# Output projection of a hybrid encoder trunk: seven block products in place of eight in half of the k pairs of five weight groups

## The reference, cut to what matters

```python
for l in range(DEPTH):                       # 2 layers, 1024 tokens, D_MODEL 2048, float32
    h = rmsnorm(x, norm_gain[l])
    proj = einsum('bsd,de->bse', h, w_in[l])     # q, k, v, g_attn, x_rnn, g_rnn
    attn = swa_sink_attention(q, k, v, sinks[l], cos, sin)
    rnn = rg_lru(causal_conv(x_rnn, ...), ...)
    mixed = concatenate([attn * silu(g_attn), rnn * silu(g_rnn)])    # 2048 wide
    x = x + einsum('bse,ed->bsd', mixed, w_out[l])                   # the change is here
return rmsnorm(x, final_gain)
```

## Time and profile before

| what | value |
|---|---|
| median of 3 runs | 2317.74 us (2317.38 to 2317.77) |
| the profiled execution | 2318.04 us |
| its span, first to last instruction | 2316.0 us |
| TensorE busy | 2308.8 us, 12970 matmuls |
| VectorE busy | 1443.1 us |
| ScalarE busy | 1270.0 us |

### The profile page before, as it was taken

The page is one execution under the profiler, slowest core; times in us unless marked ns, Lnnn a source line. Parts: engine busy times, 40 slices in busy tenths (PEclk is TensorE's granted clock), DMA queues, the critical chain, the costliest instruction groups (busy, mean ns, idle before and its releaser), DMA issues.

```text
span 2316.0 us, 34189 instructions
## 1 busy us (share of the span) xinstructions
PE 2308.8 (100%) x12970; PEld 1896.7 (82%) x12970; DVE 1443.1 (62%) x2307; ACT 1270.0 (55%) x2435; POOL 0.8 (0%) x10
## 2 busy tenths in 40 slices
PE   9999999999999999999999999999999999999999
PEld 8888888888888888888888888888888888888888
DVE  7668777434546877744475786764355478776335
ACT  7558566324456767534465676653244557665333
POOL 0000000000000000000000000000000000000000
PEclk9999999999999999999999999999999999999999
DMA  5334323333332233353334533233333333223333
GB/s 194 103 110 149 94 89 94 98 96 100 91 103 87 85 96 88 100 168 95 98 107 146 177 104 94 89 96 97 100 95 96 94 94 89 87 89 100 96 98 140
DMA packets 127028, 244.62 MB, mean 106 GB/s; under 512 B 14352, under 2 KB 18704, under 8 KB 126096
## 3 DMA queue, kind: packets, MB, share of 16 engines
q1 hardware_dynamic: 126288, 242.28, 33.5%
q10 hardware_dynamic: 576, 0.16, 0.0%
HBM read 234.00 MB, written 8.39 MB: 105 GB/s over the span
## 4 chain that ended last, share of the span: by engine, by line
PE 97%; DVE 2%; ACT 1%; issue 1%; POOL 0%; ACTq 0%; POOLq 0%
PE proj L417 91%; PE ps_at L497 1%; PE ps_at L522 1%; PE ps_at L541 1%; PE proj L433 1%; DVE wcut L979 0%; PE proj L460 0%; DVE xc L1175 0%; DVE xcut L1189 0%; DVE prob L1149 0%; ACT wcut L618 0%; ACT prob L753 0%; PE ps_at L393 0%; ACT sqr L790 0%; ACT sqr L792 0%
## 5 line engine op out<-in xcount | busy, mean ns | idle before, releaser
L417 PE MATMUL proj<-operand,wcut 128*128 128x512 f32 x9480 | 2183.4, 391 | 0.0
L417 PEld LDWEIGHTS proj<-operand,wcut 128*128 128x128 f32 x9480 | 1775.3, 188 | 380.6 <-issue 11.0
L979 DVE TENSOR_TENSOR wcut<-wraw,wcut 128x512 fp32r<-128x512 f32 x804 | 554.3, 690 | 802.8 <-ACT wcut L618 799.7
L618 ACT ACTIVATE wcut<-wraw 128x512 fp32r<-128x512 f32 x803 | 506.3, 631 | 915.2 <-PE proj L417 890.0
L753 ACT ACTIVATE prob<-ps_at,stat 128x128 f32<-128x128 f32 x256 | 89.9, 363 | 0.8
L701 ACT ACTIVATE gy<-proj 32x512 f32<-32x512 f32 x144 | 84.9, 590 | 3.8
L658 ACT ACTIVATE sqr<-x 128x512 f32<-128x512 f32 x62 | 36.8, 635 | 45.4 <-DVE x L1220 45.2
L1008 DVE TENSOR_TENSOR acc<-acc,sqr 128x512 f32<-128x512 f32 x80 | 55.2, 691 | 4.9 <-ACT sqr L658 0.2
L764 ACT ACTIVATE mixed<-ps_at 64x256 f32<-64x256 f32 x128 | 48.6, 379 | 14.3 <-PE ps_at L522 11.9
L753 ACT ACTIVATION_READ_ACCUMULATOR prob<-ps_at,stat 128x1 f32 x256 | 51.8, 202 | 0.0
L1175 DVE SCALAR_TENSOR_TENSOR xc<-xr,pars,xc 128x512 f32<-128x512 f32 x64 | 47.9, 749 | 1.4
(11 more groups left out here) (154 smaller groups left out, 1193.0 us busy)
## 6 DMA issues: line engine op xcount, KB each, us to landing
wraw<-in_w SPq DMA_DIRECT2D x804, 256.0 KB, 2.6
x<-in_xt SPq DMA_DIRECT2D x2, 4096.0 KB, 13.5
mixed<-in_xt SPq DMA_DIRECT2D x14, 512.0 KB, 7.4
gw<-in_gates SPq DMA_DIRECT2D x32, 128.0 KB, 2.6
out<-x SPq DMA_DIRECT2D x4, 1024.0 KB, 4.9
out<-mixed SPq DMA_DIRECT2D x7, 512.0 KB, 2.6
tab<-in_cossin SPq DMA_DIRECT2D x8, 256.0 KB, 3.3
mixed<-in_xt SPq DMA_DIRECT2D x4, 256.0 KB, 3.4
```

Source lines behind the costliest of these rows:

```text
L417: last = pe.matmul(bank[:, :], wcut[:, u % RING, a, c:c + P], operand[:, k, b, :], start=(k == 0 and n == 0), stop=(k == KT - 1 and n == 2))
L618: act.activation(wcut[:, u % RING, 0, :], wraw[:, u % RING, :], ACT.Copy).then_inc(w_hi, 1)
L979: dve.tensor_tensor(wcut[:, u % RING, 1, :], wraw[:, u % RING, :], wcut[:, u % RING, 0, :].bitcast(F32), ALU.subtract).then_inc(w_lo, 1)
```

## The change

Groups 19 to 23 of each layer treat four of their eight k pairs (`NSP` = 4) as a 2x2 block product: two k blocks by two output tiles, times two k blocks by two halves of 256 tokens. Eight block products of 256 tokens become seven (Strassen's form as arranged by Winograd), each still three fp32r matmuls. Four of the seven (`lead`) need sums of weight blocks and of operand blocks, and are made during the group before, in the other pair of banks; then ScalarE and VectorE add the banks across (`lead_copy_out`, `lead_sums`), and the plain k pairs and the other three products (`cross_part`) gather on top. A slot that has a cross part with it is in `SIDES`.

Group 18 has twelve slots (144 to 155): four of them, every second one, are lead parts for group 19. Groups 19 to 22 have eight each: in slots 2 to 5 of a group TensorE makes a cross part of its own group and a lead part of the next, the other four are plain. Group 23 has four plain slots, each with a cross part. So slots stay 200.

For each such k pair VectorE makes five sums of 128x128 weight blocks (`weight_sums`) in place in the raw ring, three slots ahead, before `weight_hi` may round them; two raw blocks are loaded once more (`cross`, 128 KB), and cut to high and low beside one of the sums (`cross_cut_hi`, `cross_cut_lo`), two slots ahead. The operand sums are made once per layer and half, at slots 126, 128, 136 and 143. The next half's x is loaded in two parts, at slots 148 and 195. Several buffers share memory with ones that are idle in this stage (left out below, with declarations and the index helpers).

```diff
--- before
+++ after
@@ -61,7 +61,33 @@
 STREAM = [(g, j) for j in range(5) for g in range(2)] + [(g, j) for g in range(2) for j in range(5, UPG)]
-STREAM += [(g, j) for g in range(2, PG + OG) for j in range(UPG)]
+STREAM += [(g, j) for g in range(2, PG) for j in range(UPG)]
+KIND = ["plain"] * len(STREAM)
+SIDE = [None] * len(STREAM)
+NSP = 4
+SG = list(range(PG + 2, PG + 7))
+def out_slots():
+    for g in range(PG, PG + OG):
+        plain = list(range(NSP if g in SG else 0, UPG))
+        for s in range(UPG + (g + 1 == SG[0]) * NSP - (g == SG[-1]) * NSP):
+            ahead = s - 2 if g in SG else (s - 2) // 2
+            if g + 1 in SG and ahead in range(NSP) and (g in SG or s % 2 == 0):
+                yield "ahead", g + 1, ahead, (g, ahead) if g in SG else None
+            else:
+                yield "plain", g, plain.pop(0), (g, s) if g == SG[-1] else None
+OSTART = [None] * OG + [SLOTS]
+for what, g, j, side in out_slots():
+    at = g - PG - (what == "ahead")
+    if OSTART[at] is None:
+        OSTART[at] = len(STREAM)
+    STREAM.append((g, j))
+    KIND.append(what)
+    SIDE.append(side)
...
-XS = O0 + (OG - 1) * UPG + 1
+XS = OSTART[OG - 1] + 1
+PIECE = {STREAM[s]: s for s in range(SLOTS) if KIND[s] == "ahead"}
+SIDES = [s for s in range(SLOTS) if SIDE[s]]
+NPC = len(PIECE)
+CUTS = 3
+HOLD = 5
+T_AT = (126, 128, 136, 143)
...
@@ -358,10 +428,25 @@
                             sp_.wait_ge(gw_lo, h * (DEPTH * RT) + (n + 1))
                             sp_.dma_start(gw[:, n % GRING, :, :], gates[l, j]).then_inc(gw_in[n % GRING], 16)
+                        if s + 1 in SIDES:
+                            g, i = SIDE[s + 1]
+                            n = at_piece(h, l, piece(g, i))
+                            sp_.wait_ge(xsum_lo, per_layer(h, l, NSP, 1))
+                            if n >= HOLD:
+                                sp_.wait_ge(cross_lo, n - HOLD + 1)
+                            sp_.dma_start(cross[n % HOLD][:, 0:2 * P],
+                                          w[l, PIECE[g, i], :, 2 * P:4 * P]).then_inc(cross_in[n % HOLD], 16)
                         if l == 1 and s == O0 + 12 and h < LAST:
                             sp_.wait_ge(op_lo, at_op(h, 1, 1, KT - 1))
-                            for i in range(KT // 2):
+                            sp_.wait_ge(xsum_done, per_layer(h, 1, NSP, NSP))
+                            for i in range(KT // 4):
+                                x_load(h + 1, i)
+                        if l == 1 and s == OSTART[OG - 1] + AHEAD and h < LAST:
+                            sp_.wait_ge(unit_done, at_unit(h, 1, OSTART[OG - 1] - 1))
+                            for i in range(KT // 4, KT // 2):
                                 x_load(h + 1, i)
...
@@ -401,6 +486,8 @@
                 if s == 0:
                     pe.wait_ge(evac, h * (DEPTH * TILES) + (l * TILES + 2))
+                if g in SG and s == OSTART[g - PG]:
+                    pe.wait_ge(lead_done, 3 * (lead_at(h, l, g) + 1))
                 pe.wait_ge(w_lo, h * UNITS + (u + 1))
...
@@ -410,13 +497,47 @@
                         bank = proj[2 * ((l * (PG + OG) + g) % 2) + m]
                         c = kk * GW + m * P
                         for n, (a, b) in enumerate(((0, 0), (0, 1), (1, 0))):
-                            if (kk, m, n) == (KU - 1, 1, 2) and s + 1 < SLOTS and STREAM[s + 1][1] == 0:
+                            if ((kk, m, n) == (KU - 1, 1, 2) and s + 1 < SLOTS and STREAM[s + 1][1] == 0
+                                    and KIND[s + 1] == "plain"):
                                 pe.wait_ge(evac, h * (DEPTH * TILES) + (l * TILES + 2 * STREAM[s + 1][0] + 2))
                             last = pe.matmul(bank[:, :], wcut[:, u % RING, a, c:c + P], operand[:, k, b, :],
-                                             start=(k == 0 and n == 0), stop=(k == KT - 1 and n == 2))
-                last.then_inc(unit_done, 1)
+                                             start=(k == 0 and n == 0), stop=(k == KT - 1 and n == 2),
+                                             skip_group_check=g in SG)
+                return last
+            def lead(h, l, s):
+                u = l * SLOTS + s
+                g, i = STREAM[s]
+                k1 = KU * i
+                banks = bank_of(l, 2 * g), bank_of(l, 2 * g + 1)
+                if i == 0:
+                    pe.wait_ge(evac, h * (DEPTH * TILES) + (l * TILES + 2 * g + 2))
+                if g == SG[0]:
+                    pe.wait_ge(xsum_lo, per_layer(h, l, NSP, i + 1))
+                pe.wait_ge(w_lo, h * UNITS + (u + 1))
+                for c, b, m, half in ((0, None, 0, 0), (3, 1, 0, 1), (2, 2, 1, 0), (1, 0, 1, 1)):
+                    for n, (hi, lo) in enumerate(((0, 0), (0, 1), (1, 0))):
+                        src = operand[:, k1, lo, 0:HT] if b is None else xsum[i][:, lo, b, :]
+                        last = pe.matmul(banks[m][:, HT * half:HT * half + HT], wcut[:, u % RING, hi, P * c:P * c + P],
+                                         src, start=(i == 0 and n == 0 and half == 0),
+                                         stop=(i == NSP - 1 and n == 2), skip_group_check=True)
+                return last
+            def cross_part(h, l, g, i):
+                n = at_piece(h, l, piece(g, i))
+                k2 = KU * i + 1
+                pe.wait_ge(cross_lo, n + 1)
+                cut = crosscut[n % CUTS]
+                for c, b, m, half in ((0, 0, 0, 0), (2, 1, 0, 1), (1, None, 1, 0)):
+                    for hi, lo in ((0, 0), (0, 1), (1, 0)):
+                        src = operand[:, k2, lo, HT * b:HT * b + HT] if b is not None else xsum[i][:, lo, 3, :]
+                        last = pe.matmul(bank_of(l, 2 * g + m)[:, HT * half:HT * half + HT], cut[:, hi, P * c:P * c + P],
+                                         src, start=False, stop=False, skip_group_check=True)
+                return last
...
@@ -549,7 +670,13 @@
                         elif h == 0 and l == 0 and s == 0:
                             first_units()
                         elif h > 0 or l > 0 or s > 1:
-                            unit(h, l, s)
+                            if KIND[s] == "plain":
+                                last = unit(h, l, s)
+                            if SIDE[s]:
+                                last = cross_part(h, l, *SIDE[s])
+                            if KIND[s] == "ahead":
+                                last = lead(h, l, s)
+                            last.then_inc(unit_done, 1)
                         if h > 0 and l == 0 and s == SS_OUT:
                             sum_of_squares(h - 1, DEPTH)
...
@@ -615,7 +742,31 @@
                     act.wait_ge(unit_done, u - RING + 1)
                 if u == 1:
                     act.wait_ge(w_hi, 1)
+                if u < TOTAL and KIND[u % SLOTS] == "ahead":
+                    act.wait_ge(wsum_done, at_piece(u // UNITS, u // SLOTS % DEPTH, piece(*STREAM[u % SLOTS])) * 2 + 2)
                 act.activation(wcut[:, u % RING, 0, :], wraw[:, u % RING, :], ACT.Copy).then_inc(w_hi, 1)
+            def cross_cut_hi(h, l, g, i):
+                n = at_piece(h, l, piece(g, i))
+                act.wait_ge(cross_in[n % HOLD], 16 * (n // HOLD + 1))
+                act.wait_ge(wsum_done, 2 * n + 2)
+                if n >= CUTS:
+                    hb, r = divmod(n - CUTS, DEPTH * NPC)
+                    act.wait_ge(unit_done, at_unit(hb, r // NPC, SIDES[r % NPC]))
+                act.activation(crosscut[n % CUTS][:, 0, :], cross[n % HOLD], ACT.Copy).then_inc(cross_hi, 1)
+            def xsum_cut_hi(h, l, i):
+                act.wait_ge(xsum_done, per_layer(h, l, NSP, i + 1))
+                if i >= 2:
+                    act.wait_ge(op_lo, at_op(h, l, 1, AT + RT // 2 * (i - 1) - 1))
+                act.activation(xsum[i][:, 0, :, :], xraw[i][:, :, :], ACT.Copy).then_inc(xsum_hi, 1)
+            def lead_copy_out(h, l, g):
+                act.wait_ge(unit_done, at_unit(h, l, PIECE[g, NSP - 1]))
+                act.activation(xc[:, 0:HT], bank_of(l, 2 * g)[:, 0:HT], ACT.Copy).then_inc(lead_copy, 1)
...
@@ -837,10 +988,17 @@
                 for l in range(DEPTH):
                     for s in range(SLOTS):
                         u = h * UNITS + l * SLOTS + s
+                        for g in SG:
+                            if s == PIECE[g, NSP - 1] + 1:
+                                lead_copy_out(h, l, g)
+                        if s + 2 in SIDES:
+                            cross_cut_hi(h, l, *SIDE[s + 2])
                         if u > 0 and u + AHEAD < TOTAL:
                             weight_hi(u + AHEAD)
                             act.wait_ge(w_hi, u + AHEAD + 1)
+                        if s - 1 in T_AT:
+                            xsum_cut_hi(h, l, T_AT.index(s - 1))
                         for p in range(NP):
                             if s == VAL[p] + 1:
...
@@ -979,6 +1137,66 @@
```

(96 more changed lines are left out.)

15 lines of the change are left out of this document (9 added, 6 removed).

## The result

| | median us | ratio to before (95%) |
|---|---|---|
| before | 2317.56 | |
| after | 2378.99 (2378.17 to 2379.26) | 1.0265 (1.0247 to 1.0282) |

What follows compares the result with a forecast made beforehand. TensorE, 97% of the chain, was taken to bound the kernel; 58.3 us of new pauses less 16.3 us of saved matmul work gave +42 on 2318.0, so 2360 us. Own range 2340 to 2382, with rivals 2330 to 2394.

Steps and rivals of the forecast that it cites:

- TensorE's own work: 80 k pairs, each going from 12 long matmuls (2.72 us) to 21 short ones (2.52 us): 16.3 us less.
- The price of the sums: VectorE's 128-column sums: 0.29 us each by a straight line between neighbours; the five of weight_sums 1.46 us.
- A serial chain of VectorE and ScalarE through slots 6, 7, 0 to 3: At group changes, sums, cuts, residuals and squares run in a row and make TensorE pause: 58.3 us in all.
- Its length: Chain from slot 5's end to next slot 5's end: 24.2 us against TensorE's 21.0, pausing 3.2 us per first-layer group.
- What lies beside other work: Operand sums, group 18's short slots, SyncE's extra 128 KB load per pair and x's bulk load: taken at no cost.
- signs of being wrong: TensorE without such idle time, a chain ending on lead sums or a weight load by DMA, short matmuls at another pace.
- The second layer costs more: Gains between squares and cross cut raise the pause per group from 3.2 to 4.45 us; early squares add some 3.9 us.
- The bulk load: x's load delays weights in group 18's short lead slots: nothing to 1.5 us, once; taken as nothing.
- The operand sums at no cost: Four per layer and half, around slots 126 to 143: VectorE has room or low cuts stay over 4 us ahead; costed nothing.
- Short work is cheap: Rival: all five weight sums at the 16-column price, 33 us less, 2327 us; chance 0.08.
- the chain is longer by dear sums: Rival: each weight sum at the 256-column price, 39 us more, 2399 us; chance 0.12 with milder forms.
- the cuts stay hidden: Rival: VectorE's chain in slots 7 to 2 fits into 21.0 us, TensorE never pauses, 2302 us; chance 0.05.

Runs made afterwards that it cites:

- e8: Kernel after with weight sums on GpSimd and one slot earlier, cross load two slots earlier, squares, gains and sums of squares of groups 18 to 21 four slots later: 2304.6 us.
- e2: Kernel after with the cross load issued two slots earlier on SyncE, nothing else: 2366.3 us.
- e1: Kernel after without three of the five weight sums of each k pair, so its output differs: 2330.5 us.
- e3: Kernel after with each weight_sums moved behind its slot's low cut, four slots ahead instead of three, one more cross buffer: 2340.9 us.
- e6: Kernel after with weight sums one slot earlier, cross load two slots earlier, squares, gains and sums of squares of groups 18 to 21 four slots later: 2312.6 us.
- e5c: e2 plus fill-in matmuls, 10 and 3 a group ahead of two long waits, in groups 20 to 22 only: 2364.6 us.

## Why the prediction was right, and where it was off

- *TensorE's own work: right.* 16.3 us less were predicted. e8 shows 20.98 us a group (the prediction's 21.0; a short matmul at 0.120 us, not at the 0.109 of the estimate beside it) and 13.2 us in all. Of the difference 1.1 is one wait for late weights behind the bulk load of x (a slot pair of 5.30 us where others take 4.18), half a microsecond lies in groups 18 and 23, where a long matmul beside a short one costs a little (3.82 for 3.80, 4.18 for 4.16); the rest, 1.5, I can't place.
- *The price of the sums: right.* 0.292 us against 0.29, and a set of five takes 1.47. (The prediction's own terms, 3 x 0.325 + 0.215 + 0.29, add up to 1.48 and not to the 1.46 it goes on with, 1 us in all. Its row for a signal, 450.07 to 450.81 after 0.63 of work, gives 0.11, not 0.09 to 0.10, and the run has some 0.04 from ScalarE's cut to VectorE's. The slot of 2.98 came out as 2.98 even so (e2, 476.12 to 479.10), in part by luck.) The 0.19 us worked out from the table in the Trainium skill, "VectorE: DVE Perf Modes", section on the TRN2 errata, is not borne out by it; the note under that table, (N+151)/0.96 ns for a float32 sum, gives 0.291 and is.
- *A serial chain of VectorE and ScalarE through slots 6, 7, 0 to 3: right*, place by place, and shown by e1, e3 and e6: shorter, reordered, or relieved of the squares, it gives the time back. TensorE's idle time is released by the low cross cut, as said, in slots 4 and 5 of the group shown; of the low weight cut, named as the second releaser, there is next to nothing (0.3 us).
- *Its length: too short.* From the trace, groups 19 to 22 hold 75.0 us of pauses and slowed matmuls in the four passes; 58.3 were predicted. The failed step is in "What lies beside other work": SyncE's load of 128 KB was given "two more waits, each on something a group old" and no time. Its semaphores are old, but it is issued in order behind the raw load of its slot, which waits for the low cut at the end of slot 6; so it starts 3 us after T and lands at 6.3, and slot 0's cross cut begins at 6.96 where I had 6.38. With it out of the way (e2) the cut begins at 6.20, the pauses sum to 62.6 us, and the kernel takes 12.7 us less. Not all of that is the load's own wait: the kernel after has nine stretches of low clock and e2 five, and at e5c's 0.4 us each, as an estimate, 1.6 of the 12.4 us between the sums are clock. The low clock, which I had not in the sum at all, is 1.6 us of e2's pauses (e5c) and, by the same estimate, 3.6 of those in the kernel after. What is left, 61.0 against 58.3, is in part the first nine matmuls after a pause, 1.34 us in place of 1.08; I did not split the rest.
- *Luck in the number.* 2379.0 lies within my own 2340 to 2382, but that range was made for dearer sums and refills. The sums came as forecast; what filled its upper part was the load, which I had taken at nothing. One of my signs of being wrong showed as well, a load by DMA in the chain (2% of the span).
- *The second layer costs more: right.* Groups took 25.0 to 25.3 us in the first, 26.2 to 27.4 in the second (24.2 and 25.4 predicted, and more with early squares; those in the second layer passed the "24 to 26 us" of the signs).
- *The bulk load:* a pause of 0.5 us in group 18, once; within the "nothing to 1.5".
- *The operand sums at no cost: right.* In each of the four passes TensorE takes the same time as before, within 0.2 us, from the layer's first slot to slot 144, two slots ahead of the first lead part.
- *The rivals.* "Short work is cheap" and "the chain is longer by dear sums" fell on the measured 0.292. That the cuts stay hidden was wrong for this kernel, but the price from which it would turn was right in kind: e6 takes nearly 2 us a group out of the chain beyond e3's reordering, and the kernel turns faster.

## What to carry to other kernels

When an engine cuts, sums or rounds operands ahead of TensorE, add its work up slot by slot in program order, with every wait on a partner engine, and compare with TensorE's time for those slots; a busy share of 62% hid a stretch in which 24 us of serial work stood against 21. Before giving up a change that loses there, move work that is not urgent (squares, gains) out of the stretch, give sums a slot of lead so that nobody waits inside a slot, and use an idle engine, though its work beside VectorE's made both slower here: the same algebra went from 61 us slower to 13 us faster.

For a DMA, look at what its queue waits for ahead of it, not only at its own waits.

## What the runs showed of the hardware that was not expected

After 2.26 us without a matmul TensorE ran on at full clock for about a microsecond and then for 3.4 us at 1.2 GHz; after the same pause one group earlier it did not. Yet in these kernels such a stretch cost only about 0.4 us, as most of what it lost lay ahead of a wait.

GpSimd's `tensor_tensor` of 128x128 float32 took 0.59 us on average and 0.45 at its shortest. While one was in work, VectorE's low cuts took longer, 0.783 in place of 0.689 us at 512 columns and 0.701 in place of 0.556 at 384; a mean over the whole span (0.698) hides it.
